# Attention of a two-layer encoder trunk: both heads' value products of a pair in one group that alternates between two column halves, q and v read where they lie, and the pairs written out

## The reference, cut to what matters

```python
for q0 in range(0, S, Q_BLOCK):          # S = 512, Q_BLOCK = 128
    q1 = q0 + Q_BLOCK
    s = einsum('bhqd,bhkd->bhqk', q[:, :, q0:q1], k[:, :, :q1]) * scale
    if cum is not None:                  # FoX only
        s = s + cum[:, :, q0:q1, None] - cum[:, :, None, :q1]
    s = where(mask, s, -inf)
    p = softmax(s, axis=-1)
    outs.append(einsum('bhqk,bhkd->bhqd', p, v[:, :, :q1]))
```

## Time and profile before

| what | value |
|---|---|
| median of 3 runs (lowest to highest) | 1842.99 us (1842.26 to 1843.1) |
| span of the profiled execution | 1840.4 us |
| median less span | 2.6 us |
| TensorE busy in the span | 1783.4 us (97%) |
| VectorE busy in the span | 1111.3 us (60%) |
| TensorE's granted clock, all 40 slices | 9 (90% or more of full speed) |
| attention stages, first value of their logits to the end of their last products | 4, together 239.2 us |

### The profile page before, as it was taken

How to read it: one execution, slowest core, us unless ns; L and a number is a source line. 1 busy time by engine, 2 the same in 40 slices (tenths; PEclk the granted TensorE clock), 3 DMA queues, 4 the chain that set the end, 5 groups by cost and what they waited for, 6 DMA issues and landing times.

```text
span 1840.4 us, 25304 instructions
## 1 busy us (share of the span) xinstructions
PE 1783.4 (97%) x7905; PEld 1402.4 (76%) x7905; DVE 1111.3 (60%) x1681; ACT 718.1 (39%) x1185; POOL 199.2 (11%) x170
## 2 busy tenths in 40 slices
PE   5999999999999999999999999999999999999997
PEld 4775775877888888888878658578778888888886
DVE  7688786767555555543348869767565455555333
ACT  4456335534343323222235552554333433232222
POOL 3232001001011000001120410100100200000011
PEclk9999999999999999999999999999999999999999
DMA  4430320333333333333332213113233333333332
GB/s 121 106 70 12 81 69 1 89 89 91 89 112 97 98 93 101 92 94 95 96 88 65 63 27 94 29 41 98 80 95 111 92 101 92 97 96 93 93 102 78
DMA packets 311125, 153.21 MB, mean 83 GB/s; under 512 B 30532, under 2 KB 309310, under 8 KB 311052
## 3 DMA queue, kind: packets, MB, share of 16 engines
q1 hardware_dynamic: 310752, 152.10, 29.7%
q10 hardware_dynamic: 300, 0.19, 0.0%
HBM read 150.14 MB, written 2.10 MB: 83 GB/s over the span
## 4 chain that ended last, share of the span: by engine, by line
PE 82%; DVE 9%; issue 5%; ACT 3%; DVEq 0%; DMA 0%; ACTq 0%; SPq 0%
PE bank L1282 74%; PE bank L1356 4%; PE bank L1333 2%; PE bank L1344 2%; ACT w_hi L614 1%; DVE w_lo L896 1%; DVE p_b L967 1%; ACT p_b L657 1%; DVE c_acc L956 1%; DVE h_lo L925 0%; DVE neg_max L974 0%; PE bank L1307 0%; DVE c_raw L1085 0%; PE bank L1486 0%; DVE rstd_kv L930 0%
## 5 line engine op out<-in xcount | busy, mean ns | idle before, releaser
L614 ACT CAST w_hi<-raw 128x1024 fp32r<-128x1024 f32 (+3 forms) x364 | 308.2, 859 | 847.3 <-PE bank L1282 846.4
L1282 PE MATMUL bank<-h_hi,w_hi 128*128 128x512 f32 (+1 forms) x1504 | 594.6, 395 | 9.9 <-DVE w_lo L896 5.0
L1282 PE MATMUL bank<-h_hi,w_lo 128*128 128x512 f32 (+1 forms) x1504 | 586.5, 390 | 0.0
L1282 PE MATMUL bank<-h_lo,w_hi 128*128 128x512 f32 (+1 forms) x1504 | 586.2, 390 | 0.0
L896 DVE TENSOR_TENSOR w_lo<-raw,w_hi 128x1024 fp32r<-128x1024 f32 (+3 forms) x364 | 360.3, 1000 | 242.6 <-ACT w_hi L614 239.8
L1282 PEld LDWEIGHTS bank<-h_hi,w_hi 128*128 128x128 f32 (+1 forms) x1504 | 282.1, 188 | 81.9 <-issue 19.9
L1282 PEld LDWEIGHTS bank<-h_lo,w_hi 128*128 128x128 f32 (+1 forms) x1504 | 282.3, 188 | 60.4 <-issue 2.5
L1282 PEld LDWEIGHTS bank<-h_hi,w_lo 128*128 128x128 f32 (+1 forms) x1504 | 282.1, 188 | 60.1
L917 DVE TENSOR_TENSOR tmp<-bank,rstd_x 128x512 f32<-128x512 f32 x160 | 110.5, 691 | 302.8 <-PE bank L1282 301.3
L956 DVE SCALAR_TENSOR_TENSOR c_acc<-u_pad,dwk_l,c_acc 128x512 f32<-128x512 f32 x240 | 178.7, 773 | 1.0
L488 POOL TENSOR_TENSOR x_acc<-x_acc,x_sq 128x512 f32<-128x512 f32 x40 | 67.6, 1690 | 893.2 <-ACT x_sq L624 892.7
(11 more groups left out here) (187 smaller groups left out, 1888.0 us busy)
## 6 DMA issues: line engine op xcount, KB each, us to landing
raw<-in_w_in SPq DMA_DIRECT2D x98, 512.0 KB, 3.8
raw<-in_w_ffn_gate SPq DMA_DIRECT2D x44, 512.0 KB, 3.8
raw<-in_w_ffn_up SPq DMA_DIRECT2D x44, 512.0 KB, 3.8
raw<-in_w_ffn_down SPq DMA_DIRECT2D x32, 512.0 KB, 3.6
raw<-in_w_out SPq DMA_DIRECT2D x16, 512.0 KB, 3.6
raw<-in_w_ffn_down SPq DMA_DIRECT2D x16, 384.0 KB, 3.2
raw<-in_w_bo_a SPq DMA_DIRECT2D x16, 256.0 KB, 2.8
raw<-in_w_bo_b SPq DMA_DIRECT2D x16, 256.0 KB, 2.8
```

The costliest lines, as they stand in the source:

```text
L614: last = nc.scalar.copy(to, of)
L1282: ins = nc.tensor.matmul(bank_t[0:rows, :], wt[slot][:, w], x, start=first and k == 0 and p == 0, stop=last and k == k_tiles - 1 and p == 2)
```

## The change

The pairs are written out on all engines in place of the loops, so a pair's number is known when the program is built. With that, `logits` reads `q_t` and `values` reads `v_n` directly, and POOL's copies into `q_st` and `v_st` go, with their semaphore. For FoX, POOL now sets row 64 of all eight heads of `q_t` to one in a single instruction.

There are now two buffers `p_t`, one for each head of a pair. `values` runs once for a pair, behind turn 1 of the next pair, and behind the last turn for the last pair. It alternates: for each key tile k, first the product of head e = 0 into rows 0 to 63 of `o_bank`, then that of head e = 1 into rows 64 to 127. Only the copy of turn 0 (no longer that of turn 4) waits for products.

```diff
-    p_t = at("p_t", r0 + 77 * KB, [P, TT, T])
-    q_st = [at(f"q_st{i}", r0 + (85 + 2 * i) * KB, [P, T]) for i in range(2)]
+    p_t = [at(f"p_t{e}", r0 + 77 * KB + 4 * e * P_T_SIZE, [P, TT * P_T_STEP + 3 * P]) for e in range(2)]
...
-            def attention(rows, hi_out, lo_out):
-                pool.wait_ge(evac_done, evac.value)
-                passed(pool)
-
-                def stage(pair, first):
-                    for e in range(2):
-                        if not first:
-                            pool.wait_ge(score_done, score.value - 4 + 4 * e)
-                            passed(pool)
-                        nc.gpsimd.tensor_copy(q_st[e][0:rows, :], head_of(q_t, pair, e)[0:rows, :]).then_inc(st_ready, 1)
...
-                    nc.gpsimd.tensor_copy(v_st[:], v_n[:, :, bass.ds(pair * P, P)]).then_inc(st_ready, 1)
...
+            def attention(hi_out, lo_out):
+                for pair in range(PAIRS):
                     pool.wait_ge(o_hi_done, ohi.add())
...
-                for e in range(2):
-                    nc.gpsimd.memset(q_st[e][NOPE:NOPE + 1, :], 1.0).then_inc(ones_put, 1)
...
+                nc.gpsimd.memset(q_t[NOPE:NOPE + 1, :, :], 1.0).then_inc(ones_put, 1)
...
                 def turn(s, first=False):
                     act.wait_ge(turn_done, tn.add())
-                    if s % 4 == 0:
-                        if not (first and s == 0):
+                    if s == 0:
+                        if not first:
                             act.wait_ge(pv_done, pv.value)
                         pv.add()
...
                 def pair_out(pair):
-                    act.wait_ge(pv_done, ohi.add(2))
+                    act.wait_ge(pv_done, ohi.add())
...
-                def values(e, ago):
-
-                    if e == 0:
-                        pe.wait_ge(o_hi_done, pairs_in.value)
-                        pairs_in.add()
-                        pe.wait_ge(st_ready, st.value + 3)
+                def values(pair, ago):
+
+                    pe.wait_ge(o_hi_done, pairs_in.value)
+                    pairs_in.add()
+                    if pair == 0:
+                        pe.wait_ge(v_ready, vr.value)
                     pe.wait_ge(turn_out, to.value - ago)
 
                     for k in range(TT):
-                        ins = nc.tensor.matmul(o_bank[e * VDIM:(e + 1) * VDIM, k * P:T], v_st[:, k, e * VDIM:(e + 1) * VDIM],
-                                               p_t[:, k, k * P:T], start=(k == 0), stop=True, skip_group_check=True)
+                        for e in range(2):
+                            head = 2 * pair + e
+                            ins = nc.tensor.matmul(o_bank[e * VDIM:(e + 1) * VDIM, k * P:T], v_n[:, k, head * VDIM:(head + 1) * VDIM],
+                                                   p_t[e][:, k * (P_T_STEP + P):k * P_T_STEP + T], start=(k == 0), stop=True,
+                                                   skip_group_check=True)
                     ins.then_inc(pv_done, 1)
...
-                        if s == 0 and not first:
-                            values(1, 1)
-                        if s == 4:
-                            values(0, 1)
+                        if s == 1 and pair:
+                            values(pair - 1, 2)
```

More of the change, by code:

```diff
@@ L566, in _ @@
                                             rope_t[rows, g // 4 * 2 + 1, :], ALU.add).then_inc(rope_put, 1)
[L567 to L573, removed]
[L574 to L580 removed]
+                evac.add(12)
+                attention(oa_hi, oa_lo)
+                pool.wait_ge(score_done, score.add(STEPS // 2))
+                passed(pool)
+                nc.gpsimd.memset(q_t[NOPE:NOPE + 1, :, :], 1.0).then_inc(ones_put, 1)
+                attention(ob_hi, ob_lo)
+                score.add(STEPS // 2)
+                pool.wait_ge(pv_done, pv.add(HEADS))
                 passed(pool)
@@ L650, in pair_out @@
                     nc.scalar.copy(o_raw[:], o_bank[:])
-                    nc.scalar.copy(tile_of(hi_out, pair), o_bank[:]).then_inc(o_hi_done, 1)
-                def body(pair, first):
+                    nc.scalar.copy(hi_out[:, pair, :], o_bank[:]).then_inc(o_hi_done, 1)
+                for pair in range(PAIRS):
                     for s in range(8):
@@ L659, in body @@
                                              accum_out=row_sum[:, s % 4:s % 4 + 1]).then_inc(exp_done, 1)
-                        if s >= 2 or not first:
-                            turn((s - 2) % 8, first)
-                        if s == 2 and not first:
+                        if s >= 2 or pair:
+                            turn((s - 2) % 8, pair == 0)
+                        if s == 2 and pair:
                             pair_out(pair - 1)
-                body(0, True)
-                with repeat(act, PAIRS - 1, [(mx, 8), (tn, 8), (pv, 2), (ohi, 2), (olo, 1)]) as i:
-                    body(i + 1, False)
                 turn(6)
@@ L967, in normalise @@
                     nc.vector.tensor_scalar(p, p, row_inv[:, s % 4:s % 4 + 1], None, ALU.mult).then_inc(norm_done, 1)
-                def body(pair, first):
-                    last_tile[0] = None
+                last_tile[0] = None
+                for pair in range(PAIRS):
                     for s in range(8):
@@ L975, in body @@
                                                 negate=True).then_inc(max_ready, 1)
-                        if s > 0 or not first:
+                        if s > 0 or pair:
                             normalise((s - 1) % 8)
-                        if first and s == 6:
+                        if pair == 0 and s == 6:
                             last_split()
@@ L1327, in logits @@
                     e, q = s // 4, s % 4
+                    head = 2 * pair + e
                     pe.wait_ge(exp_done, ex.add())
-                    if q == 0:
-                        pe.wait_ge(st_ready, st.value + 1 + e)
                     w = (q + 1) * P
-                    nc.tensor.matmul(s_bank[q][:, 0:w], q_st[e][0:rows, q * P:w], head_of(k_t, pair, e)[0:rows, 0:w],
-                                     start=True, stop=True)
+                    nc.tensor.matmul(s_bank[q][:, 0:w], q_t[0:rows, head, q * P:w], k_t[0:rows, head, 0:w], start=True, stop=True)
                     nc.tensor.matmul(s_bank[q][:, q * P:w], ident_b[:], mask_b[:, kind, :], start=False, stop=True,
@@ L1389, in attention @@
                 logits(0, 2)
-                body(0, first=True)
-                with repeat(pe, PAIRS - 2, [(st, 3), (ex, 8), (nm, 8), (to, 8), (pairs_in, 1)]) as i:
-                    body(i + 1)
-                body(PAIRS - 1, last=True)
-                values(1, 0)
+                for pair in range(PAIRS):
+                    body(pair, last=(pair == PAIRS - 1))
+                values(PAIRS - 1, 0)
             pe.wait_ge(const_ok, 1)
```

58 lines of the change are left out of this document (21 added, 37 removed).

## The result

| | median us | runs | lowest to highest |
|---|---|---|---|
| before | 1842.99 | 5 | 1841.76 to 1843.52 |
| after | 1850.53 | 5 | 1847.52 to 1855.54 |

The ratio is 1.0045, 95% interval 1.0034 to 1.0056: the change makes the kernel slower by 0.45%, where 1840.6 us was predicted. The runs after scatter over 8 us, those before over 2. The profiled run took 1855.54 us, span 1853.8, so its numbers add up to somewhat more than the median.

The account below looks back on a forecast made before the run. TensorE looked nearly the bound, but its gain would mostly become waits for VectorE. Pairs of G + 10.0 and the stage ends gave four stages of 236.8 us against 239.2; span 1838.0 plus 2.6 made 1840.6 us, range 1834 to 1867.

Parts of the forecast that it names:

- G: Length of a pair's one group of value products for both heads on TensorE, taken as 2.9 us.
- rival 2: Full overlap of both heads' value products: group of 2.30 us, 9.6 us less, 1831 us; chance 0.06.
- B1: First product record of the second head in the value group, issued third; claimed to run beside A2.
- A1: First product record of the first head in the value group, which A2 needs finished.
- A2: Second product record of the first head, issued between A1 and B1; claimed to need A1 finished.
- A group under 2.5 us: Sign set in advance that would prove the forecast wrong, for the value group of both heads.
- G + 10.0: Time from group to group, in us: G + 3.01 + 6.62 + 0.05 + 0.22 + 0.10; 13.1 before.
- The sum: Attention stages: MLA 47.9 + 4G, FoX 47.3 + 4G; all four 190.4 + 16 x 2.9 = 236.8 us.
- G + 12.84: Last pair of a stage: third group G, then 12.84 us to the start of the last group.
- VectorE's list: VectorE's fixed work, said to set the first pair's pace: first group 15.1 us behind MLA's start, 14.5 in FoX.
- The rival of the other sign: Halves do not run together: 1.54 us more in each of 16 groups, 24.6 us, 1865.2 us; chance 0.25.
- The other edits: POOL copies, ones, written-out loops, `p_t` stride: costed at 0, except 0.35 us of slow VectorE multiplication per first pair.

Follow-up runs that it names:

- Experiment 2: Changed kernel with the loops in `values` swapped, so all four products of one head come first, then the other's: 1875.39 us.
- Experiment 1: Changed kernel plus idle TensorE products in its waits, 9 in each stage's first pair and 8 in each later pair: 1834.42 us.
- experiment 3: Changed kernel plus idle TensorE products in the first pair of each stage alone, 9 of them: 1837.46 us.
- experiment 5: Changed kernel with VectorE's split of the dense chunk's low half moved behind the stage's last normalisation: 1840.87 us.
- experiment 6: Changed kernel with ScalarE taking exp 3 ahead of its copy of turn 0 in pairs 1 to 3: 1830.83 us.
- number 7: Changed kernel with both the dense split late and exp 3 ahead of the copy of turn 0: 1817.21 us.
- experiment 4: Changed kernel's written-out pairs and q, v read in place, but one `p_t` and two groups per pair as before: 1840.02 us.

## Why the prediction was wrong, by its own steps

**The group: mis-sized.** G was set at 2.9 us, rival 2 at 2.30 got a chance of 0.06. It measured 2.30. The argument was that B1 cannot run beside A1 because A2 is issued in between. The trace shows the loads at the group's start as x4 within 0.20 us and then in pairs: both heads' records start together, step by step. The Trainium skill ("TensorE: Matmul & The Clock Gate", Part 3) gives a ratio of 2.38 for three column tiles, and my estimate of 2.8 us, shared out from it for two, came out too long. No run here has three tiles; two halves took 4.60 us in two groups and 2.30 in one, a factor of two. A group under 2.5 us was set as the sign that would prove the forecast wrong, and it came. Experiment 2 shows that the order matters, as I had said: 3.86 us. By itself this error made the forecast too slow, by 16 x 0.6 = 9.6 us; it is not why the kernel came out slower.

**The pair: right.** G + 10.0 was the formula; 12.40 - 2.30 = 10.1. The chain behind it came out piece by piece: 3.14 us from the products' end to turn 3 predicted, 3.09 measured; VectorE's wait for exp 3 about 3, measured 2.86; turn 3's wait about 1.6, measured 1.29. TensorE's waits in the first MLA stage, as the view of waits has them (total, times, longest), are 8.4 us together where some 10 were expected, from 3.4:

```profile
PE bank L1299 <- DVE p_b L928: 4.5, 12, 1.3
PE bank L1299 <- ACT p_t L609: 3.9, 3, 1.3
```

**The sum: right once the clock is held.** With G = 2.30 it is 190.4 + 36.8 = 227.2 us for the four stages. Experiment 1, at full clock, has 230.1, so each stage is 0.7 us longer than worked out. Of that 0.5 lies in the last pair: 15.67 us between the starts of its two groups, against G + 12.84 = 15.14. It is the price of the idle products: the changed kernel has 196.25 - 181.08 = 15.17 there. The MLA stage at full clock of experiment 3, which has idle products in its first pair only, takes 57.17 us, where 47.9 + 9.2 = 57.1 was worked out. Rival 2's 1831 us stands beside 1834.42 measured.

**What failed: the clock, taken as 1.00.** No step of the prediction asked what the change does to it, though the text foresaw longer waits on TensorE. I counted the first head's products of the first pair as work that moves, and the first group's start from VectorE's list alone; that these products had been the cover over the dense split, and that without them TensorE stands idle for 1.33 us in a pair with little work, was missed. The fall costs at least 249.8 - 230.1 = 19.7 us in the profiled run, which turns a gain of 9 into a loss of 10.6 in the stages; without the idle products' own price the fall's cost and the gain would each be some 2 us more. Experiments 1, 5, 6 and 7 show it from four sides: filling the waits, removing either, and removing both. The rival of the other sign (halves not together, 1865) named the right direction for a reason that is not there; the measured time lies in the range by that luck.

**The other edits: small, not nothing.** Costed at 0 but for 0.35 us in each first pair, they gave 2.6 us in experiment 4 and 3.3 in its stages (239.2 to 235.9). The 0.35 is there: the two groups of its first pairs are 6.02 us apart, 6.37 before. The pair takes 12.96 instead of 13.1 us, 12 times 0.14 = 1.7 us; 0.11 of the 0.14 is the multiplication of step 3, which lasts 0.72 us there and 0.83 before, for a reason not looked into; the prediction had found a slow multiplication in the first pair only.

**Outside the stages.** No change was forecast, and one had been named as a sign against the forecast; the span outside them went from 1840.4 - 239.2 = 1601.2 to 1604.0 us. In experiment 4 it is 1602.9, so 1.7 of these 2.8 us come without the group. In it 0.7 lies between the two stages of the layers (61.3 to 61.7 us each, as in experiments 4 and 7), 0.9 between the layers and 1.6 behind the last stage; 0.4 is gained ahead of the first. Of the 1.6 us, 0.8 stand in the kernel's last 14 us, where the granted clock is at 0.50 for 10 us at a time instead of 3.4; it is so in experiments 1, 3, 4 and 6 too and not in 2, 5 and 7, so it does not follow the attention's waits. The cause of the rest stays open.

Left open as well: why the same waits bring the clock down mostly in FoX and seldom in MLA. In the traces of the changed kernel and of experiments 2, 3, 5 and 6, the MLA stages have 30 waits of 1.29 to 1.33 us and 4 falls behind them, the FoX stages 30 and 17. Why one such wait is followed by a fall and the next is not stays open too; it differs even between the two MLA stages of one execution (experiment 2). No run here separates the two kinds of stages.

## What to carry to other kernels

Before work is taken off TensorE beside a slower engine, read which waits it covered, and count a fall of the granted clock as a rival with its own price. If the clock row of the page shows a dip after a change, put idle products into the waits for one run; it tells what the change is worth without it, less the idle products' own price. Then remove the waits themselves: here that was worth 33 us, where the idle products brought 16, since it shortens the chain as well.

## What the hardware showed that was not expected

- Two column halves whose fp32 products alternate take 2.30 us for both heads, exactly one head's time; in turn they take 3.86.
- A single wait of 1.29 to 1.33 us could be followed by the half clock: 4 of 30 such waits in MLA stages, 17 of 30 in FoX. The fall outlasts the wait: 3.4 us each time in MLA, in the changed kernel's first FoX stage from 271 to 281 us and from 285 to 298. It began between 0.2 us before and 2.5 us after the end of the wait.
- Waits of up to 0.99 us (the longest in number 7's first stage, ahead of turn 5 of its last pair) were followed by no fall in any of its four stages.
